# Recurrent heads: two of each head's four modulation chunks scaled and added up on GpSimd, TensorE adds only the partitions

## The reference, cut to what matters

```python
mod = jax.nn.silu(cvec) @ w + b              # first block: [1, 1024] @ [1024, 6 * 1024]
return jnp.split(mod[:, None, :], N_MOD, axis=-1)
...
cond = jax.nn.silu(c)                        # second block, for each of two layers
mod = cond @ w_ada[i] + b_ada[i]
```

## Time and profile before

| | |
|---|---|
| timed runs, median (lowest to highest) | 3184.11 us (3183.24 to 3185.1) |
| the profiled execution: its own time | 3186.0 us |
| its span, first to last instruction | 3184.1 us |
| TensorE / VectorE / ScalarE / GpSimd busy | 95% / 47% / 23% / 0% of the span |
| engines' shares of the chain that ended last | PE 84%, DMA 6%, DVE 4%, ACT 2% |
| heads 0 to 6 (114.84 to 583.20 us of the span) | 468.4 us, TensorE busy 465.0 |
| head 7 and the joint products (to 660 us) | 76.8 us, TensorE busy 73.2 |

### The profile page before, as it was taken

The page is one execution under the profiler, slowest core; times in us unless marked ns, Lnnn a source line. Parts: engine busy times, 40 slices in busy tenths (PEclk is TensorE's granted clock), DMA queues, the critical chain, the costliest instruction groups (busy, mean ns, idle before and its releaser), DMA issues.

```text
span 3184.1 us, 37185 instructions
## 1 busy us (share of the span) xinstructions
PE 3030.5 (95%) x15055; PEld 2232.9 (70%) x15055; DVE 1501.4 (47%) x2423; ACT 737.1 (23%) x1397; POOL 15.9 (0%) x30
## 2 busy tenths in 40 slices
PE   6999999999999999979999998899999998999999
PEld 4888888868855888854444443468888855788887
DVE  2577766725566445451101123256544525745544
ACT  4243433321067110120000012232000024300001
POOL 0000000000000000000000000000000000000000
PEclk8999999999999999989999998999999999999999
DMA  5144434332200132248999991102222211122221
GB/s 225 61 191 182 156 139 166 133 144 81 106 12 10 54 132 80 80 164 359 421 422 422 422 380 56 66 1 80 93 93 80 81 80 54 54 80 80 81 104 54
DMA packets 64235, 451.81 MB, mean 142 GB/s; under 512 B 7248, under 2 KB 7264, under 8 KB 11216
## 3 DMA queue, kind: packets, MB, share of 16 engines
q1 hardware_dynamic: 61200, 439.38, 34.5%
q0 software_dynamic: 2080, 7.11, 0.7%
q10 hardware_dynamic: 800, 3.15, 0.3%
HBM read 445.41 MB, written 2.10 MB: 141 GB/s over the span
## 4 chain that ended last, share of the span: by engine, by line
PE 84%; DMA 6%; DVE 4%; ACT 2%; issue 1%; PEld 1%; DVEq 1%; SPq 0%; PEldq 0%; POOL 0%; ACTq 0%; POOLq 0%
PE PS L228 77%; DMA ring<-stream 5%; PE PS L1621 1%; PE PS L1508 1%; PEld PS L228 1%; PE PS L1604 1%; DVE arena L1573 1%; DMA hT<-stream 1%; DVE stat L1630 1%; PE PS L2296 1%; PE PS L2276 1%; ACT arena L1526 0%; DVE PS L2622 0%; PE PS L2279 0%; PE PS L873 0%
## 5 line engine op out<-in xcount | busy, mean ns | idle before, releaser
L228 PE MATMUL PS<-arena 128*128 128x256 f32 (+3 forms) x4960 | 986.1, 389 | 9.0 <-issue 4.9
L228 PEld LDWEIGHTS PS<-arena 128*128 128x128 f32 (+1 forms) x4960 | 744.1, 183 | 237.8 <-issue 156.6
L228 PE MATMUL PS<-arena,ring 128*128 128x256 f32 (+1 forms) x1992 | 467.5, 391 | 0.3 <-issue 0.3
L228 PE MATMUL PS<-hT,ring 128*128 128x256 f32 (+1 forms) x1504 | 413.6, 431 | 23.6 <-ACT hT L323 11.5
L228 PEld LDWEIGHTS PS<-arena,ring 128*128 128x128 f32 x1992 | 377.9, 190 | 75.4 <-issue 27.3
L228 PEld LDWEIGHTS PS<-hT,ring 128*128 128x128 f32 x1504 | 291.2, 195 | 132.4 <-issue 88.3
L228 PE MATMUL PS<-xT,arena 128*128 128x256 f32 x1056 | 232.0, 379 | 0.0
L228 PEld LDWEIGHTS PS<-xT,arena 128*128 128x128 f32 x1056 | 200.6, 190 | 28.1 <-issue 1.0
L228 PE MATMUL PS<-ring,arena 128*32 128x512 f32 (+3 forms) x1088 | 198.5, 590 | 12.3 <-issue 6.4
L228 PE MATMUL PS<-hT,arena 128*128 128x256 f32 (+1 forms) x864 | 195.2, 442 | 1.3 <-DMA hT<-stream 1.3
L2095 DVE TENSOR_TENSOR arena<-arena,PS 128x512 f32<-128x512 f32 x16 | 11.0, 688 | 368.4 <-PE PS L228 368.4
(11 more groups left out here) (307 smaller groups left out, 2942.4 us busy)
## 6 DMA issues: line engine op xcount, KB each, us to landing
ring<-stream SPq DMA_DIRECT2D x283, 1024.0 KB, 6.9
arena<-stream SPq DMA_DIRECT2D x96, 1024.0 KB, 18.8
hT<-stream SPq DMA_DIRECT2D x32, 1024.0 KB, 18.8
arena<-stream SPq DMA_DIRECT2D x8, 512.0 KB, 4.9
arena<-x ACTq DMA_DIRECT2D x1, 2048.0 KB, 10.2
xT<-stream SPq DMA_DIRECT2D x2, 1024.0 KB, 15.6
arena<-arena POOLq DMA_DIRECT2D x16, 128.0 KB, 2.6
arena<-x POOLq DMA_DIRECT2D x1, 2048.0 KB, 12.7
```

The costliest lines, as they stand in the source:

```text
L228: ins = nc.tensor.matmul(out_, lhsT, rhs, start=start, stop=stop_, **kw)
```

## The change

The tuple POOLED says how many of a head's four chunks GpSimd takes: two in heads 0 to 6, none in head 7. For these (`ada_pool`), GpSimd waits for each unit of the chunk, multiplies each of its four 128 x 512 blocks in place by the conditioning value of the partition (one scalar per partition), and adds the blocks up: two pairs at once, then the two sums, into a buffer of 128 x 512. Chunk 0 has `ada_part` for this, chunk 1 the buffer of `ada_row`. SP may load the first unit of the next chunk once the first half of a GpSimd chunk is done (`w_half`), the second once the whole is done (now GpSimd raises `w_pair[1]`).

TensorE leaves out these chunks. It starts bank 5 with chunk 2, and behind chunk 3's eight products it waits for GpSimd (`a_g`) and adds two products whose stationary operand `sel1` has a single column of ones; they add up the partitions of the two buffers into rows 0 and 1 of strips 0 and 1. Two semaphores of the routing stage are merged, and the arena grows by 100 floats per partition.

```diff
--- before.py
+++ after.py
@@ -50,6 +50,7 @@
 
 
 ADA0 = 4
+POOLED = (2,) * 7 + (0,)
 NQ = 2 + 6
 N_MERGE = HG + NQ
 N_OUT = N_MERGE + 12
@@ -161,7 +162,7 @@
         rstd = sb("rstd", [P, T])
         pt = sb("pt", [P, 2, T])
         st8 = sb("st8", [P, 32])
-        arena_n = 33100
+        arena_n = 33200
         arena = sb("arena", [P, arena_n])
         PS = ctx.enter_context(nc.psum_tensor("PS", [P, 8, 512], fp32))
 
@@ -195,10 +196,11 @@
         w_used = sem("w_used")
         w_pair = [sem(f"w_pair{p}") for p in range(3)]
         w_vals = sem("w_vals")
+        w_half, a_g = sem("w_half"), sem("a_g")
         mm_done = sem("mm_done")
         evac_done = sem("evac_done")
-        in_const, in_vec, in_x, in_c, in_cst2, in_acst, in_iota = (sem(n) for n in
-            ("in_const", "in_vec", "in_x", "in_c", "in_cst2", "in_acst", "in_iota"))
+        in_const, in_vec, in_x, in_c, in_cst2, in_acst, in_route = (sem(n) for n in
+            ("in_const", "in_vec", "in_x", "in_c", "in_cst2", "in_acst", "in_route"))
         vec_t, vec_ok, cs_ok, ada_sel = (sem(n) for n in ("vec_t", "vec_ok", "cs_ok", "ada_sel"))
         mods_ok = sem("mods_ok")
         n_x, n_ac, n_sq, n_ss, n_r, n_h, n_mod = (sem(n) for n in ("n_x", "n_ac", "n_sq", "n_ss", "n_r", "n_h", "n_mod"))
@@ -445,6 +447,8 @@
         Sp = area(at, 3, KH, HN); at += 3 * KH * HN
         Xp = area(at, 2, 2, HN); at += 4 * HN
         Up = area(at, 2, 2, HN); at += 4 * HN
+        ada_part = area(at, 512); at += 512
+        sel1 = area(at, 36); at += 36
         T_x = xflat.rearrange("p (a b c) -> p a b c", a=4, b=KH)
         qT = area(6144, KT, T)
         hKo = hL
@@ -555,6 +559,9 @@
         def start_dve(v):
             nc.vector.memset(st8[:, 31:32], EPS)
             nc.vector.memset(csq[:, :, :, :], 0.0)
+            nc.vector.memset(sel1[:, 0:3], 0.0)
+            nc.vector.memset(sel1[:, 3:4], 1.0)
+            nc.vector.memset(sel1[:, 4:36], 0.0)
             nc.vector.memset(cs[:, :, :], 0.0)
             v.drain().then_inc(cs_ok, 1)
             norm_dve(v, 0, x0, hT)
@@ -808,20 +815,54 @@
 
             return OA[:, HG - 1, :] if h < HG - 1 else hz[:, 0, 0:T]
 
+        def ada_acc(h, c):
+
+            return ada_part if c == 0 else OA[:, HG - POOLED[h] + c, :]
+
+        def ada_pool(pool, h):
+
+            which = 0 if h < HG - 2 else 1
+            for c in range(POOLED[h]):
+                u, acc = UNIT_OF["A", 4 * h + c], ada_acc(h, c)
+                if h:
+                    pool.wait_ge(a_p, 2 * h - 1 if c == 0 else 2 * h)
+                for half in range(2):
+                    unit_wait(pool, u + half)
+                    w = ring[slot(u + half)][:, :].rearrange("p (k n) -> p k n", n=512)
+                    for k in range(4):
+                        nc.gpsimd.tensor_scalar(w[:, k, :], w[:, k, :], csq[:, which, 4 * half + k, 3:4], None, ALU.mult)
+                    pool.drain()
+                    nc.gpsimd.tensor_tensor(w[:, 0:2, :], w[:, 0:2, :], w[:, 2:4, :], ALU.add)
+                    pool.drain()
+                    if half == 0:
+                        nc.gpsimd.tensor_tensor(acc, w[:, 0, :], w[:, 1, :], ALU.add).then_inc(w_half, 1)
+                    else:
+                        nc.gpsimd.tensor_tensor(acc, acc, w[:, 0, :], ALU.add)
+                        pool.drain()
+                        nc.gpsimd.tensor_tensor(acc, acc, w[:, 1, :], ALU.add).then_inc(w_pair[1], 1)
+            pool.drain().then_inc(a_g, 1)
+
         def ada_products(pe, h, c):
 
-            u = UNIT_OF["A", 4 * h + c]
+            u, by_pool = UNIT_OF["A", 4 * h + c], POOLED[h]
             which = 0 if h < HG - 2 else 1
-            if c == 0:
+            if c == min(by_pool, 3):
                 pe.wait_ge(p_d, 4 * (h + 1 if h < HG - 1 else HG + 1) + 2)
-            for k in range(KT):
-                q, su = k % 4, u + k // 4
-                if q == 0:
-                    unit_wait(pe, su)
-                mm(PS[32 * q:32 * q + 32, 5, :], csq[:, which, k, 3 - c:35 - c],
-                   ring[slot(su)][:, q * 512:(q + 1) * 512], c == 0 and k < 4, c == 3 and k >= 4,
-                   a_p if c == 3 and k == KT - 1 else None, tile_position=(0, 32 * q))
-            places.append(w_pair[slot(u) // 2])
+            if c >= by_pool:
+                for k in range(KT):
+                    q, su = k % 4, u + k // 4
+                    if q == 0:
+                        unit_wait(pe, su)
+                    last = c == 3 and k >= 4 and q >= by_pool
+                    mm(PS[32 * q:32 * q + 32, 5, :], csq[:, which, k, 3 - c:35 - c],
+                       ring[slot(su)][:, q * 512:(q + 1) * 512], c == by_pool and k < 4, last,
+                       a_p if last and k == KT - 1 and not by_pool else None, tile_position=(0, 32 * q))
+                places.append(w_pair[slot(u) // 2])
+            if c == 3 and by_pool:
+                pe.wait_ge(a_g, h + 1)
+                for q in range(by_pool):
+                    mm(PS[32 * q:32 * q + 32, 5, :], sel1[:, 3 - q:35 - q], ada_acc(h, q), by_pool == 4, True,
+                       a_p if q == by_pool - 1 else None, tile_position=(0, 32 * q))
 
         def ada_sums(pe, h):
 
@@ route_pe / route_dve
...
-            pe.wait_ge(in_router, 16)
+            pe.wait_ge(in_route, 32)
...
-            v.wait_ge(in_iota, 16)
+            v.wait_ge(in_route, 32)
...
@@ -2668,7 +2709,7 @@
                 sp.dma_start(ring[slot(u)][:, 0:n], stream[u, :, 0:n]).then_inc(w_loaded[SIGNAL[slot(u)]], 16)
 
             sp.wait_ge(in_x, 16)
-            taken = [0, 0, 0, 0]
+            taken, halved, by_pool = [0, 0, 0, 0], 0, False
             for name, i, place in EARLY:
                 u = UNIT_OF[name, i]
                 if name == "v":
@@ -2676,11 +2717,19 @@
                         sp.wait_ge(w_vals, i)
                     load(u, UNIT // 2)
                     continue
-                if taken[place]:
+                if place == 1 and by_pool:
+                    halved += 1
+                    sp.wait_ge(w_half, halved)
+                    load(u)
                     sp.wait_ge(w_pair[place], taken[place])
+                else:
+                    if taken[place]:
+                        sp.wait_ge(w_pair[place], taken[place])
+                    load(u)
                 taken[place] += 1
-                load(u)
                 load(u + 1)
+                if place == 1:
+                    by_pool = name == "A" and i % 4 < POOLED[i // 4]
             for u in range(U_MERGE, N_UNITS):
                 if U_EXP + 10 <= u < U_EXP + WIDE:
                     sp.wait_ge(mm_done, G_H2T + 8)
@@ -2702,14 +2751,17 @@
             pool.dma_start(v_rows, vecs).then_inc(in_vec, 16)
 
             pool.dma_start(H_CST, hcst).then_inc(in_cst2, 16)
+            pool.wait_ge(cs_ok, 2)
+            for h in range(HG - 1):
+                ada_pool(pool, h)
             pool.wait_ge(h_out, HG + 1)
             pool.dma_start(A_CST, acst.rearrange("p (a b) -> p a b", a=2)).then_inc(in_acst, 16)
             swap_halves(pool, gqa_scores)
             pool.wait_ge(p_p, 7 * (N_MERGE + 4))
             pool.dma_start(x_again, x.rearrange("(m p) d -> p m d", p=P)).then_inc(in_x2, 16)
             pool.wait_ge(x_ok, 1)
-            pool.dma_start(iota_s, iota).then_inc(in_iota, 16)
-            pool.dma_start(rw, router).then_inc(in_router, 16)
+            pool.dma_start(iota_s, iota).then_inc(in_route, 16)
+            pool.dma_start(rw, router).then_inc(in_route, 16)
             pool.wait_ge(x_ok, 2)
             pool.dma_start(posi, pos).then_inc(in_pos, 16)
             pool.wait_ge(x_ok, 4)
```

More of the change, by code:

```diff
@@ L1855, in build @@
         idxu = sb("idxu", [NE, CAP], u32)
-        in_router, r_lg, r_sum, r_mx, r_ex, r_aff, r_affT, r_tt, r_blk, r_row, r_ok = (sem(n) for n in
-            ("in_router", "r_lg", "r_sum", "r_mx", "r_ex", "r_aff", "r_affT", "r_tt", "r_blk", "r_row", "r_ok"))
+        r_lg, r_sum, r_mx, r_ex, r_aff, r_affT, r_tt, r_blk, r_row, r_ok = (sem(n) for n in
+            ("r_lg", "r_sum", "r_mx", "r_ex", "r_aff", "r_affT", "r_tt", "r_blk", "r_row", "r_ok"))
         e_g, e_xs, e_gu, e_sg, e_hid, e_T, e_hT, e_dn, e_ys, e_cb, e_acc = (sem(n) for n in
```

## The result

The changed kernel takes 3240.73 us in the median (3237.91 to 3243.29, four runs), the kernel before 3184.61 beside it: ratio 1.0184, 95% interval 1.0170 to 1.0198. It is 1.8% slower. Forecast was 3175 and a gain; the range ended at 3208.

A forecast was written before the change was run, and what follows sets the result against it. TensorE's order and an equally long chain (context end, load, VectorE, output) bound the heads. 13.0 + 0.7 + 2.1 − 6.65 = 9.1 us saved gave 3176.9, as median 3175.0; range 3167 to 3208.

The forecast's parts named there:

- GpSimd's price: GpSimd's scalings and additions per chunk, priced from VectorE's rows: 8.4 to 17.5 us, the middle 13 taken.
- If GpSimd runs undisturbed: Condition on GpSimd's chunk work: both chunks done in time even at 17.5 us each, by 222 against 226.6.
- rival A: GpSimd and VectorE exclude each other at the levels, 0.83 us a hold: 3199 us, at the upper price 3223; chance 0.20.
- 1.85 of cover: Head's output: TensorE arrives 1.85 us earlier and waits there; 1.85 is taken off a late GpSimd's cost.
- rival B: GpSimd too late for chunk 2: 21 us a chunk, 17 of exclusion, some 17 a head, 3300 us; chance 0.07.
- The deadline: Chunk 2's load in head 1: GpSimd must finish by 226.6, as TensorE wants it at 233.9 and landing takes up to 7.3.
- Chunk 0 worth 1.85: Chunk 0's eight products, ahead of the context projection and on both chains: saves 1.85 us a head, 13.0 in seven.
- chunk 1 nothing: Chunk 1's products, behind the context's end: TensorE waits 1.85 us at the output instead; 0.7 saved in all.
- Added products: Two new TensorE products over GpSimd's sums, overlapping: cost 0.95 us a head, 6.65 in seven.
- Chunk 3's DMA wait: The fourth chunk's late second unit: its load gains 1.85 us, saving 0.3 a head, 2.1 in all.
- SP, the rotary table's DMA, memsets, routing: SP's load queue, GpSimd's queued DMA, three starting VectorE memsets, merged routing semaphores: cost 0 each; routing below 1 us at worst.
- VectorE beside GpSimd: VectorE's two-input work on the next head's factors: holds of 4.2 us fit in 4.8 of slack, cost 0.

The follow-up runs named there:

- one-chunk form: Changed kernel with GpSimd taking only chunk 0 of each head (POOLED one instead of two), its full work kept: 3175.97 us, 0.9980 to the kernel before.
- that with half the scalings: Changed kernel, but GpSimd scales only two of each unit's four blocks, all additions kept, values not the true ones: 3200.88 us, 1.0061.
- exchanging their places: One chunk a head, GpSimd one addition per unit (values not true), TensorE's chunk products kept at chunk 0's place, not chunk 1's: 3188.38 us, against 3175.46 unexchanged.
- two-chunk forms with GpSimd in time: Changed kernel with GpSimd's work cut, values not true: one addition per unit without scalings, 3178.41 us; all scalings with one addition per unit, 3174.68 us.

## Why the prediction was wrong

*GpSimd's price: the step that failed.* "I take the middle, 13", with 17.5 as the upper end, from VectorE's rows. Alone a chunk is 20.7. The scan's 2.28 ns an element was right for GpSimd's additions (2.26 to 2.4) and wrong for the scaling (3.0), eight of thirteen instructions. The estimate of 17 in the prediction doubled VectorE's scalings too, though what it cites speaks of two-input additions: these took 1.8 and 1.9 times VectorE's, the scaling 3.2 times.

*"If GpSimd runs undisturbed": the other half of that step.* In head 1 the chunks took 28.2 and 25.2 us, 12 more than two alone. The forecast had nothing for this; it stood only in rival A, as 17. An estimate from these numbers: at 20.7 undisturbed both chunks are done at 228.3 (186.9 + 41.4), 1.7 past 226.6, which by the prediction's terms the 1.85 of cover hides; at 13 with the 12 on top they are done at 225. It took both to come to 240.3, and with the start at 189.15 instead of 186.9 to 242.5.

The kernel measured is rival B (21 a chunk, 17 of exclusion, done near 246), with a chance of 0.07. B's 17 us a head was too high: GpSimd was done 3.5 us earlier, the landing took 4.8 and not 7.3, and TensorE first lacked the second unit, at 236.7 and not 233.9, so the wait was 10.6.

*The deadline* of 226.6, and that chunk 2 would be where TensorE waits: right. In the one-chunk form and that with half the scalings this wait is gone.

*Chunk 0 worth 1.85, chunk 1 nothing:* right as a sum, shown by exchanging their places, 12 us. The mechanism of chunk 1's nothing was right only in part: the forecast let VectorE's states take its 1.85 us back at the output, and chunk 2's load takes the larger part. *Added products* 0.95: measured 0.96. *Chunk 3's DMA wait* gone: in the changed kernel in all but two heads (0.9 us in all, before 1.45 in four); in the two-chunk forms with GpSimd in time chunk 2 waits for its load instead, 9 to 10 us in all, so the 2.1 are not there. *SP, the rotary table's DMA, memsets, routing:* nothing seen.

*VectorE beside GpSimd "within the slack", 0:* at the levels right for the changed kernel but for head 0 (1.8 + 1.2 us); at the output right by luck, for VectorE came 4.3 us later there and only the late chunk 2 hid it. Rival A had 0.83 for each hold: it is 0.2 for a scaling and an addition's whole length. With GpSimd in time, the full additions cost 3.4 us a head (68.8 against 65.4) and the two-input scalings 6.7 (72.3 against 65.6). That VectorE's addition waits for the end of GpSimd's (1.77 us instead of 0.68) agrees with the Trainium skill ("SBUF — State Buffer", Who interferes with whom); beside GpSimd's scaling it does not (0.86), and there the measurement decides.

*TensorE's clock* after a long wait, 2.1 us a head, stood in no term.

## What to carry to other kernels

Before work goes to an idle engine, price its instructions there; another engine's rows are no bound, and if a rival just beyond the assumed bound flips the sign, the bound is the thing to doubt. What counts is how long the moved work holds what others need (here a ring pair, cycle 28 + 25 + loads against a head of 66), not how busy the engine is. And GpSimd additions beside VectorE are paid by VectorE: with the scalings and a single addition per unit (not the true values) two chunks gained 0.25%, with a faster two-input instruction one chunk lost 1.3%. A wait can also hide a second one: ask what the engine would wait for next if the first were cured.

## What the runs showed of the hardware

A GpSimd product of 128x512 float32 with one scalar per partition takes 1.545 us, an addition of two tensors 1.23; with the scalar broadcast as a second tensor the product took 1.50 and 1.52 us in the heads, on the mean of two runs, where the other form took 2.05 and 2.30. Beside GpSimd additions a VectorE addition of two SBUF tensors took 1.77 instead of 0.68 us, and a VectorE scaling with one 1.56 instead of 0.49; beside GpSimd scalings they took 0.86 and 0.75. After 10.6 us of waiting TensorE's granted clock read 0.50 and the next 2.7 us ran at it. In the form with the exchanged place, head 1, it read 0.50 from 239 to 241 us after waits of 0.51 and 1.61 us.
